# Feed-forward in two phases with up products by Strassen's scheme, in a two-block network on one Trainium2 core

## The reference

```python
def conv_ffn(h, w_up, conv_w, conv_b, w_down):          # h 1024 x 1024, D_FF = 2816
    u = h @ w_up
    gate, val = u[..., :D_FF], u[..., D_FF:]
    gp = jnp.pad(gate, ((0, 0), (1, 1), (0, 0)))
    gate = gp[:, :-2] * conv_w[0] + gp[:, 1:-1] * conv_w[1] + gp[:, 2:] * conv_w[2] + conv_b
    return (jax.nn.silu(gate) * val) @ w_down
...
        x = x + gate_m * rmsnorm_2(y, g_post_mix[i])
        h = modulate(rmsnorm_2(x, g_pre_ffn[i]), shift_f, scale_f)
        x = x + gate_f * rmsnorm_2(conv_ffn(h, ...), g_post_ffn[i])
```

## Time and profile before

| | us |
|---|---|
| median of 3 runs | 4103.11 |
| lowest and highest | 4101.33, 4105.68 |
| the profiled execution | 4098.11 |
| its span, first to last instruction | 4096.3 |
| TensorE, VectorE, ScalarE, GpSimd busy | 3646.1, 2173.3, 1411.1, 1411.5 |
| mean granted TensorE clock | 0.93 |

### The profile page before, as it was taken

How to read it: one execution, slowest core, us unless ns; L and a number is a source line. 1 busy time by engine, 2 the same in 40 slices (tenths; PEclk the granted TensorE clock), 3 DMA queues, 4 the chain that set the end, 5 groups by cost and what they waited for, 6 DMA issues and landing times. The chain is left out here.

```text
span 4096.3 us, 60818 instructions
## 1 busy us (share of the span) xinstructions
PE 3646.1 (89%) x19612; PEld 3206.0 (78%) x19612; DVE 2173.3 (53%) x4637; ACT 1411.1 (34%) x3493; POOL 1411.5 (34%) x1820
## 2 busy tenths in 40 slices
PE   5999979999999993939997669999995989999996
PEld 4899767999999973828986558888884768888885
DVE  5466764556777753037775244444446344444446
ACT  1377213768777702013342121111112251111111
POOL 2365323555667625321111352222222222222221
PEclk9999989999999996969998879999997679999998
DMA  4211544111121131000000021111102021111102
GB/s 160 93 40 39 214 179 173 39 40 56 63 63 61 60 145 62 31 12 1 0 0 31 12 101 46 46 59 49 46 31 103 16 77 46 46 46 47 61 31 82
DMA packets 68770, 256.83 MB, mean 63 GB/s; under 512 B 7520, under 2 KB 34432, under 8 KB 55680
## 3 DMA queue, kind: packets, MB, share of 16 engines
q1 hardware_dynamic: 68608, 254.86, 17.0%
HBM read 221.00 MB, written 33.83 MB: 62 GB/s over the span
## 5 line engine op out<-in xcount | busy, mean ns | idle before, releaser
L1858 PE MATMUL ps<-hT_hi,up_hi 128*128 128x512 f32 x1408 | 549.9, 391 | 13.4 <-DVEq L1811 13.4
L1859 PE MATMUL ps<-hT_lo,up_hi 128*128 128x512 f32 x1408 | 549.4, 390 | 0.0
L1860 PE MATMUL ps<-hT_hi,up_lo 128*128 128x512 f32 x1408 | 549.4, 390 | 0.0
L1762 POOL TENSOR_TENSOR up_lo<-up_raw,up_hi 128x2048 fp32r<-128x2048 f32 x42 | 194.4, 4629 | 883.1 <-ACT up_hi L1783 883.1
L1821 DVE TENSOR_TENSOR x<-ps,x 128x512 f32<-128x512 f32 x704 | 455.8, 686 | 2.1 <-PE ps L1874 2.1
L340 PE MATMUL ps<-w_hi,hT_hi 128*128 128x512 f32 x848 | 336.9, 397 | 41.7 <-DVEq L356 25.9
L341 PE MATMUL ps<-w_lo,hT_hi 128*128 128x512 f32 x848 | 335.0, 395 | 0.0
L342 PE MATMUL ps<-w_hi,hT_lo 128*128 128x512 f32 x848 | 334.6, 395 | 0.0
L1858 PEld LDWEIGHTS ps<-hT_hi,up_hi 128*128 128x128 f32 x1408 | 265.4, 188 | 69.2 <-POOLq L1710 7.9
L1860 PEld LDWEIGHTS ps<-hT_hi,up_lo 128*128 128x128 f32 x1408 | 265.2, 188 | 55.3
L1859 PEld LDWEIGHTS ps<-hT_lo,up_hi 128*128 128x128 f32 x1408 | 265.3, 188 | 55.1
(11 more groups left out here) (269 smaller groups left out, 8609.0 us busy)
## 6 DMA issues: line engine op xcount, KB each, us to landing
mod_weights<-in_w_mod SPq DMA_DIRECT2D x24, 2048.0 KB, 8.5
up_raw<-in_w_up SPq DMA_DIRECT2D x44, 1024.0 KB, 4.7
down_raw<-in_w_down SPq DMA_DIRECT2D x44, 512.0 KB, 5.5
w_raw<-in_w_in_b SPq DMA_DIRECT2D x24, 768.0 KB, 4.3
group_rows<-unit_rows SPq DMA_DIRECT2D x64, 132.0 KB, 1.8
unit_rows<-group_rows SPq DMA_DIRECT2D x64, 132.0 KB, 2.1
x<-in_x SPq DMA_DIRECT2D x2, 4096.0 KB, 15.5
gate_rows<-gate SPq DMA_DIRECT2D x32, 256.0 KB, 2.9
```

Of the source, the lines that this page charges most:

```text
L1858: nc.tensor.matmul(out, a, t_hi[:, k, cols], start=(k == 0), stop=False)
L1859: nc.tensor.matmul(out, a, t_lo[:, k, cols], start=False, stop=False)
L1860: last = nc.tensor.matmul(out, b, t_hi[:, k, cols], start=False, stop=(k == KT - 1))
```

## The change

The up product h @ w_up of one tile is seen as a 2 x 2 by 2 x 2 block product: the inner width in two halves of 512, the tokens as even and odd tiles of 128, the columns as gate and value. Strassen's scheme (in Winograd's form) makes it with seven block products in place of eight, each 4 blocks x 3 = 12 matmuls of 512 columns. It needs four sums of weight blocks per tile f (`weight_sums`, on VectorE) and four sums of token blocks, once (`combine`, in the stage ahead), and seven combined operands of the tokens lie in SBUF, high and low: a matmul's moving operand is four runs of 128 columns, 28 KB apart. The results are added up in four PSUM banks and by ScalarE and VectorE, with a second set of banks for the next tile. ScalarE now rounds 3584 columns of weights a tile in three pieces, GpSimd subtracts them; the buffer of raw weights is single.

The hidden columns are written to DRAM (512 KB a tile). A second phase then runs over all 22 tiles twice, once for each half of the tokens, with the sums of 8 results in the 8 banks of PSUM to the end; ScalarE and VectorE split down weights (512 KB) and hidden columns (256 KB) as they come, and copy the banks out once. There are no additions into x and no memsets.

`Residual` is a new hand-written pipeline of 16 slots in place of `add_normed` and `turn` ahead of the first feed-forward; x is stored tile by tile. It and `PoolMix` end with the combinations: per pair of tiles, four VectorE operations of 512 columns, one ScalarE rounding of 2048, one subtraction of 1024 columns on VectorE and one on GpSimd. Per tile, `Residual` has four evictions of 128 x 128 on ScalarE and four on VectorE. The split of up tile 0 moves from these stages into the feed-forward; its load stays in them.

In `PoolMix` the window matrices are now stationary and the tokens move, in 256-column matmuls, 22 for a middle tile. So the result is not transposed and 8 transposes per tile are added (lag 8), with copies before and a split after them; mixing (lag 10) is of three rounded matmuls per block, 24 per tile, its PSUM banks single. The bias is loaded to one partition, w_pool is split (ScalarE 2048 columns, VectorE 2048 columns, slots 6 and 7). There are 26 slots.

The diff, cut to its core:

```diff
+def combine(core, dve, own, j):
+    b11, b21, b12, b22 = own
+    dve.tensor_tensor(b11, b12, b11, ALU.subtract).then_inc(core.combined.sem, 1)
...
+    dve.tensor_tensor(b12, b22, b12, ALU.subtract).then_inc(core.combined.sem, 1)
...
+    dve.tensor_tensor(b22, b22, b11, ALU.subtract).then_inc(core.combined.sem, 1)
...
+    dve.tensor_tensor(b21, b22, b21, ALU.subtract).then_inc(core.combined.sem, 1)
...
+    A11, A12, S3, A22, S1, S2, S4 = range(7)
+    B11, B21, B22, T1, T4, T3, T2 = range(7)
+    ORDER = ((A11, B11, 0, True, 1), (S2, T2, 1, True, 2), (S1, T1, 2, True, 2), (A12, B21, 0, False, 1), (S3, T3, 1, False, 3),
+             (S4, B22, 2, False, 2), (A22, T4, 3, True, 3))
...
+                    sp.wait_ge(core.up_lo.sem, core.up_lo.at(3 * f + 3))
+                    combined.load(sp, w_up, f + 1)
+                if not isinstance(f, int) or f > 0:
+                    sp.wait_ge(core.hidden.sem, core.hidden.at(f))
+                    sp.dma_start(hidden_dram[f - 1], cv[:, 1 - s]).then_inc(stored[1 - s].sem, 16)
...
+            def low(f, s):
+                for n, (a, b, src) in enumerate(((0, 2, raw[:, 0:2]), (4, 7, sums[:]), (2, 4, raw[:, 2:4]))):
+                    pool.wait_ge(core.up_hi.sem, core.up_hi.at(3 * f + n + 1))
+                    pool.nop(nofuse=True)
+                    pool.tensor_tensor(flat(lo, s)[:, a * QUARTER:b * QUARTER], src.rearrange("p q n -> p (q n)"),
+                                       flat(hi, s)[:, a * QUARTER:b * QUARTER].bitcast(F32), ALU.subtract).then_inc(core.up_lo.sem, 1)
...
+            def step(act, f, s):
+                act.wait_ge(core.products.sem, core.products.at(7 * f + 1))
...
+                act.activation(pairs(gate, 0), by_pairs(bank(s, 0)), ACT.Copy).then_inc(core.parts_act.sem, 1)
...
+                    high(f + 1, 1 - s, 0)
+                act.wait_ge(core.products.sem, core.products.at(7 * f + 3))
...
+                act.activation(pairs(val, 1), by_pairs(bank(s, 2)), ACT.Copy).then_inc(core.parts_act.sem, 1)
...
+                    high(f + 1, 1 - s, 1)
+                    high(f + 1, 1 - s, 2)
...
+                act.wait_ge(core.parts_dve.sem, core.parts_dve.at(5 * f + 3))
...
+                act.activation(cv[:, s], gate[:].rearrange("p j h t -> p (j h t)"), ACT.Identity, scale=conv[:, 1, bass.ds(f, 1)],
+                               bias=conv[:, 3, bass.ds(f, 1)]).then_inc(core.gate_mid.sem, 1)
+                act.wait_ge(core.gate_used.sem, core.gate_used.at(2 * f + 2))
+                act.activation(cv[:, s], cv[:, s], ACT.Silu).then_inc(core.expo.sem, 1)
...
+            def weight_sums(f):
+                a11, a12, a21, a22 = (raw[:, n] for n in range(4))
+                s1, s2, s4 = (sums[:, n] for n in range(3))
+                s3 = a21
+                dve.wait_ge(core.raw0.sem, core.raw0.at(16 * f + 16))
+                need(dve, core.up_lo, 3 * f - 1)
+                dve.tensor_tensor(s1, a21, a22, ALU.add).then_inc(core.weight_sums.sem, 1)
+                dve.wait_ge(core.weight_sums.sem, core.weight_sums.at(4 * f + 1))
+                dve.tensor_tensor(s3, a11, a21, ALU.subtract).then_inc(core.weight_sums.sem, 1)
+                dve.tensor_tensor(s2, s1, a11, ALU.subtract).then_inc(core.weight_sums.sem, 1)
+                dve.wait_ge(core.weight_sums.sem, core.weight_sums.at(4 * f + 3))
+                dve.tensor_tensor(s4, a12, s2, ALU.subtract).then_inc(core.weight_sums.sem, 1)
+            def step(dve, f, s):
+                if not final(f):
+                    weight_sums(f + 1)
+                dve.wait_ge(core.products.sem, core.products.at(7 * f + 2))
...
+                dve.tensor_tensor(pairs(gate, 1), by_pairs(bank(s, 1)), pairs(gate, 0), ALU.add).then_inc(core.parts_dve.sem, 1)
+                dve.wait_ge(core.products.sem, core.products.at(7 * f + 5))
...
+                dve.tensor_tensor(pairs(val, 0), by_pairs(bank(s, 1)), pairs(gate, 0), ALU.add).then_inc(core.parts_dve.sem, 1)
+                dve.wait_ge(core.products.sem, core.products.at(7 * f + 6))
...
+                dve.tensor_tensor(pairs(gate, 1), by_pairs(bank(s, 2)), pairs(gate, 1), ALU.add).then_inc(core.parts_dve.sem, 1)
...
+                dve.tensor_tensor(pairs(val, 1), pairs(val, 0), pairs(val, 1), ALU.add).then_inc(core.parts_dve.sem, 1)
...
+                dve.wait_ge(core.gate_mid.sem, core.gate_mid.at(f + 1))
+                dve.scalar_tensor_tensor(c[:, 1:TOK], g[:, 0:TOK - 1], w0(f), c[:, 1:TOK], ALU.mult, ALU.add).then_inc(core.gate_used.sem, 1)
+                dve.wait_ge(core.gate_used.sem, core.gate_used.at(2 * f + 1))
+                dve.scalar_tensor_tensor(c[:, 0:TOK - 1], g[:, 1:TOK], w2(f), c[:, 0:TOK - 1], ALU.mult, ALU.add).then_inc(core.gate_used.sem, 1)
+                dve.wait_ge(core.products.sem, core.products.at(7 * f + 7))
...
+                dve.tensor_tensor(pairs(val, 0), pairs(val, 0), by_pairs(bank(s, 3)), ALU.subtract).then_inc(core.parts_dve.sem, 1)
...
+                dve.wait_ge(core.expo.sem, core.expo.at(f + 1))
+                dve.tensor_tensor(c, c, val[:].rearrange("p j h t -> p (j h t)"), ALU.mult).then_inc(core.hidden.sem, 1)
...
+            def split(h, f, s):
+                n = h * FT + f
+                dve.wait_ge(core.down_hi.sem, core.down_hi.at(2 * n + 1))
+                dve.tensor_tensor(down_lo[:, s], down_raw[:, s], down_hi[:, s].bitcast(F32), ALU.subtract).then_inc(core.down_lo.sem, 1)
+                dve.wait_ge(core.down_hi.sem, core.down_hi.at(2 * n + 2))
+                dve.tensor_tensor(h_lo[:, s], h_raw[:, s], h_hi[:, s].bitcast(F32), ALU.subtract).then_inc(core.down_lo.sem, 1)
...
+            def step(pe, f, s):
+                for n, (w, z, b, start, part) in enumerate(ORDER):
+                    pe.wait_ge(core.up_lo.sem, core.up_lo.at(3 * f + part))
+                    if n == 0:
+                        need(pe, core.parts_act, 3 * f - 3)
+                    elif start:
+                        need(pe, core.parts_dve, 5 * f - 10 + (2, 3, 5)[b - 1])
+                    elif b == 1:
+                        pe.wait_ge(core.parts_dve.sem, core.parts_dve.at(5 * f + 1))
+                    else:
+                        pe.wait_ge(core.parts_act.sem, core.parts_act.at(3 * f + (1, 0, 2)[b]))
+                    out, again = bank(s, b), {} if start else {"skip_group_check": True}
+                    for k in range(4):
+                        a_hi, a_lo = hi[s][:, w, k], lo[s][:, w, k]
+                        nc.tensor.matmul(out, a_hi, combined.moving(0, z, k), start=(start and k == 0), stop=False, **again)
+                        nc.tensor.matmul(out, a_hi, combined.moving(1, z, k), start=False, stop=False, **again)
+                        last = nc.tensor.matmul(out, a_lo, combined.moving(0, z, k), start=False, stop=(k == 3), **again)
+                    last.then_inc(core.products.sem, 1)
...
+            for h in range(2):
+                def down(pe, f, s):
+                    pe.wait_ge(core.down_lo.sem, core.down_lo.at(2 * (h * FT + f) + 2))
...
+                        out, t, cols = core.ps[:, b, :], slice((b // 2) * P, (b // 2) * P + P), slice((b % 2) * 512, (b % 2) * 512 + 512)
+                        nc.tensor.matmul(out, h_hi[:, s, t], down_hi[:, s, cols], start=begin, stop=False)
+                        nc.tensor.matmul(out, h_hi[:, s, t], down_lo[:, s, cols], start=False, stop=False)
+                        last = nc.tensor.matmul(out, h_lo[:, s, t], down_hi[:, s, cols], start=False, stop=end)
...
-                    for k in range(4 * half, 4 * half + 4):
-                        out, g, cols = ps[:, half, (k % 4) * P:(k % 4 + 1) * P], k // 2, slice(k * P, (k + 1) * P)
-                        nc.tensor.matmul(out, H[:, m % 5, cols], B[:, g, kind], start=True, stop=False)
+                    for g in (2 * half, 2 * half + 1):
+                        out, cols = ps[:, half, (g % 2) * 256:(g % 2) * 256 + 256], slice(g * 256, (g + 1) * 256)
+                        nc.tensor.matmul(out, B[:, g, kind], H[:, m % 4, cols], start=True, stop=False)
...
+            m = self.tile_at(i, 8)
+            if m is not None:
...
+                for k in range(KT):
+                    last = nc.tensor.transpose(ps[:, 2 + k // 4, (k % 4) * P:(k % 4 + 1) * P], self.d_rows[:, m % 2, k * P:(k + 1) * P],
+                                               core.ident[:])
+                last.then_inc(core.d_turned.sem, 1)
...
-                            last = nc.tensor.matmul(bank[:, (g % 2) * 256:(g % 2) * 256 + 256], self.d[:, m % 2, 2 * g + k], self.w[:, g, k],
-                                                    start=False, stop=(k == 1 and g % 2 == 1))
+                            out, hi, lo = bank[:, (g % 2) * 256:(g % 2) * 256 + 256], self.d_hi[:, m % 2, 2 * g + k], self.d_lo[:, m % 2, 2 * g + k]
+                            nc.tensor.matmul(out, hi, self.w_hi[:, g, k], start=False, stop=False)
```

(17 more changed lines are left out.)

826 lines of the change are left out of this document (514 added, 312 removed).

## The result

The changed kernel takes 4027.5 us (median of 4 runs, 4024.0 to 4032.4) against 4102.3 of the kernel before on the same chip: ratio 0.9817, 95% interval 0.9800 to 0.9834. It is faster, by 75 us where 114 were forecast. 40 us are missing, and the rest of this document is about them.

A forecast was written before the change was run, and what follows sets the result against it. TensorE was taken as the bound, chiefly in the two feed-forwards. Feed-forwards -100, stage behind attention +4 and pool -18 gave -114 us: 3984, as a median 3989, range 3945 to 4055.

The forecast's parts named there:

- VectorE's loop: Up step: the tight path through VectorE sums to 16.3 us per 19.03, 2.7 us spare; with one GpSimd collision 18.6.
- (a): Rival, up step: VectorE's loop sets it at some 20.5 us through two collisions or longer hops; +64 us, 4053; chance 0.12.
- (b): Rival, up step: GpSimd's blocks all fall into VectorE's loop, 24.4 us a step; +236 us, 4225, slower; chance 0.05.
- (c): Rival, up matmuls: the strided moving read of four runs costs its upper bound; +144 us, 4133, slower; chance 0.02.
- the turn-over: Between up and down phases: TensorE idle 6.3 us, then half clock 2.0 more, while a present wait of 2.0 goes.
- The later parts arrive while products run at half clock.: Feed-forward start: only the first split's 3.4 us per layer counts; the later parts of tile 0 add nothing.
- Covered: Steady up steps: the next tile's weight load and subtractions end before needed; 1 MB lands 4.7 us after the load starts.
- The term that was best argued: Pool: middle slots, all TensorE, fall from 17.1 us to between 8.3 and 14.7, taken as 12.
- To the first pooling 44: Pool start: 44 us to the first pooling against 39.2 before, with w_lo and the bias subtraction standing before it.
- Five turning only at 5 ... then the tail 12: Pool end: five turning-only slots at 5 us, 25, then a tail of evictions, splits and combinations, 12.
- (d): Rival, pool: stays as long or longer, a chain of slots, not matmuls; +18 to +30 us, 4007 to 4019; chance 0.14.
- the stage behind attention: Attention's end to feed-forward 0: 86.2 us becomes 90, +4, including some 9 for GpSimd operations held against VectorE; bounds -5 to +12.

## Why the prediction was right and wrong

**Right: the matmuls, and VectorE's loop.** 528 x 0.2265 = 119.6 us was the whole gain, and the spacing and the step of 19.0 us hold. So rivals (a), (b) and (c) fell; for (c) that could not be known, since no row had shown the form. The sum of the loop was right too: it left 2.7 us of spare without a collision and 0.4 with one, and the traces show 2.7 and 0.6. The collision came in every step, at 2.1 us. So (a) fell narrowly: a second such collision in the loop would have made the step some 1.5 us longer (2.1 less 0.6, an estimate; no run had two).

**Right: the turn-over.** Gap 6.57 between matmul starts where 6.3 of idle were forecast, half clock behind it, down phase 241 us against 239.2 + 2.0. That the half clock is a price of its own, which goes with the gap, did not hold: with the gap gone the down phase stayed at 241.5 us or more, as the waits for the second and third tile came in its place.

**Wrong, 15 us, 13 of them in the first steps: "The later parts arrive while products run at half clock."** This term was put at nothing. Left out were the series on GpSimd (2.4, 3.5, 2.4 us), the load of tile 1 behind its last one (5.1 us from issue to the sums that need it), and that the gate addition is queued on VectorE behind sums that wait for that load. The steady check of the same loop ("Covered") was right, as it had a step's lead; the first step has none. That these are the cause is shown in the main: the lows on VectorE took 5.5 and 2.8 us off with the first tile alone, and 7.4 and 6.4 with all.

**Wrong, 23 us: the pool.** The term that was best argued held: four slots of 12.0 us and a fifth of 11.2 where 17.1 stood. That they came out at 12 is in part luck, since slots with the same instructions took 9.7 us in the execution of another kernel, by the clock. Of the 24 us by which the sum of the slots was short (188 and 3.4 for the start, 215.6 measured from start to start), 9 lie ahead of the first pooling, 12 behind the last mixing, and 3 between.
- "To the first pooling 44": 53.1. The text named the mixing weights' subtraction as standing before it, and had 4.8 us over the 39.2 of before for this and all else. It costs 9.2 alone: VectorE waits 5.4 us for ScalarE's rounding and then works 3.5. With it moved the first pooling comes at 43.9. That this is the 44 of the forecast is chance, as the forecast had the subtraction in it.
- "Five turning only at 5 ... then the tail 12": 37 us, with 3.4 for the start 40, from the end of the last mixing; it was 52 (3255 to 3307.3). The sum charged the last pair's combination and took the others as covered. The run without combinations takes off 22.5 us, all behind the last mixing. The pairs pass through a ring of two column buffers, and a buffer is freed last by GpSimd's subtraction (the last row below); with that on VectorE the end is 4 us shorter. The ring is not all of it, as two slots fewer took off 6 to 10 us more. The changed kernel's waits in that stretch:

```profile
POOL columns_combined L2526 <- ACT columns_combined L2585: 23.6, 4, 10.6
PE ps L2717 <- ACT pool_columns L2562: 22.7, 4, 9.1
DVE columns_combined L2689 <- ACT columns_combined L2585: 13.4, 4, 5.2
ACT pool_columns L2562 <- POOL columns_combined L2526: 7.1, 2, 3.5
```

Every engine waits for another. This is rival (d), "a chain of slots and not of matmuls", at chance 0.14: right about the ends, wrong about the middle. Its price, 18 to 30 us over the forecast, is what came: 23.

**Right within 4 us: the stage behind attention.** 93.4 was forecast with the start, 95.0 measured. By the run without combinations it is 64.0 + 31.0. The sum had charged the combinations 23 (8 x 2.2 us on VectorE and 4 x 1.4 for the rounding) and, within its "some 9", GpSimd's four subtractions, so up to 32. There is a slip in it, though: its terms (8.5, 62.4, 2.5, 5.6 and 9) make 88, not 90, so that with the start it was 3.6 us short and not 1.6.

The range and the sign held. The likeliest case was too hopeful, because the sum of the ends was made of durations, while an end is made of queues.

## What to carry to other kernels

The steady loop could be forecast by counts and durations, to 0.2 us; its first pass and its last could not. Walk through step 0 with every buffer empty, and ask of each wait what else stands behind it in that engine's list. An operation that prepares something for later goes behind those the next matmul needs: one such move was worth 8 us here, another took the gap between the phases from 6.6 to 0.2. Read the spare of a loop as a distance in the trace, from the end of the operation to the start of the one that waits for it: that a kernel bears more work on an engine says nothing of it when the work stands outside the loop. Where VectorE is not the bound, work handed to GpSimd beside two-tensor VectorE operations saves it little: taking 4.2 us of work a step back cost VectorE 1.85.
